# One network, three repeated patterns rewritten: the modulation products, the norm ahead of a product, and the experts' loop

## The reference

```python
# first block, per layer l (x and, in layer 0, also ctx)
sh1, sc1, gt1, sh2, sc2, gt2 = split(silu(c) @ w_ada[l] + b_ada[l], 6)   # w_ada: 1024 x 6144
h = rms_norm(x, g_mix[l]) * (1 + sc1) + sh1
q, k, v, fourier_part, ... = split(h @ w_in[l])
o = concat(global_attention, fourier_mix, window_attention)
x = x + gt1 * (o @ w_out[l])
x = x + gt2 * swiglu(rms_norm(x, g_ffn[l]) * (1 + sc2) + sh2)            # d_ff 2816
...
x = rms_norm(x, g_final)
# second block: an even layer (differential attention, SSM, swiglu) and an odd one
# (two attentions, then a mixture of 8 experts, 2 per token):
for e in range(8):
    out += gates[:, e] * ((silu(t @ w_gate[e]) * (t @ w_up[e])) @ w_down[e])   # t = rms_norm(x, gain)
```

## Time and profile before

| | us |
|---|---|
| median of 3 runs | 3140.36 (3136.24 to 3140.94) |
| the profiled execution, its own time | 3135.54 |
| span in the profile | 3133.8 |
| PE busy | 2664.2 (85%) |
| VectorE busy | 1994.3 (64%) |
| ScalarE busy | 1071.9 (34%) |
| GpSimd busy | 201.4 (6%) |
| weights and other data moved | 543.16 MB, 173 GB/s on average |

### The profile page before, as it was taken

The page is one execution under the profiler, slowest core; times in us unless marked ns, Lnnn a source line. Parts: engine busy times, 40 slices in busy tenths (PEclk is TensorE's granted clock), DMA queues, the critical chain, the costliest instruction groups (busy, mean ns, idle before and its releaser), DMA issues. The chain is left out here.

```text
span 3133.8 us, 50194 instructions
## 1 busy us (share of the span) xinstructions
PE 2664.2 (85%) x18684; PEld 2400.9 (77%) x18684; DVE 1994.3 (64%) x3414; ACT 1071.9 (34%) x1804; POOL 201.4 (6%) x179
## 2 busy tenths in 40 slices
PE   7778898799776889686379966757999999999999
PEld 4667897699565779685379965547988988988988
DVE  6555776577764577755857744654666666666665
ACT  5333444344442444231134421221322322322322
POOL 0050000000004000061000040000000000000000
PEclk9889999899897999896589985577999999999999
DMA  9422352255562134340034440002877877877876
GB/s 354 172 81 82 130 187 106 88 185 190 192 231 76 69 144 184 126 149 14 0 122 181 173 146 1 1 32 91 320 277 274 318 276 277 317 276 277 319 272 224
DMA packets 57195, 543.16 MB, mean 173 GB/s; under 512 B 6584, under 2 KB 6904, under 8 KB 9080
## 3 DMA queue, kind: packets, MB, share of 16 engines
q1 hardware_dynamic: 53840, 529.55, 46.0%
q10 hardware_dynamic: 3248, 12.17, 1.1%
HBM read 540.55 MB, written 1.15 MB: 173 GB/s over the span
## 5 line engine op out<-in xcount | busy, mean ns | idle before, releaser
L2040 PEld LDWEIGHTS bank<-projc,ring 128*128 128x128 f32 x5632 | 654.6, 192 | 17.6 <-issue 4.5
L2040 PE MATMUL bank<-projc,ring 128*128 128x128 f32 x5632 | 655.8, 275 | 1.0 <-DVE projc L2122 1.0
L571 PE MATMUL bank<-src_hi,w_hi 128*128 128x256 f32 x1472 | 420.3, 286 | 29.4 <-DVE w_lo L844 28.2
L791 ACT ACTIVATE w_hi<-ring 128x1024 fp32r<-128x1024 f32 x264 | 278.7, 1059 | 419.8 <-PE bank L573 415.6
L572 PE MATMUL bank<-src_lo,w_hi 128*128 128x256 f32 x1472 | 419.2, 285 | 0.0
L573 PE MATMUL bank<-src_hi,w_lo 128*128 128x256 f32 x1472 | 418.9, 285 | 0.0
L844 DVE TENSOR_TENSOR w_lo<-ring,w_hi 128x1024 fp32r<-128x1024 f32 x264 | 321.7, 1220 | 100.3 <-ACT w_hi L791 99.0
L571 PE MATMUL bank<-w_hi,src_hi 128*128 128x256 f32 x896 | 268.6, 300 | 77.8 <-DVE w_lo L700 69.0
L571 PE MATMUL bank<-w_hi,act_hi 128*128 128x512 f32 x704 | 292.8, 416 | 23.5 <-DVE w_lo L844 12.5
L571 PEld LDWEIGHTS bank<-src_hi,w_hi 128*128 128x128 f32 x1472 | 285.0, 194 | 35.4 <-DVE w_lo L844 30.3
L572 PEld LDWEIGHTS bank<-src_lo,w_hi 128*128 128x128 f32 x1472 | 285.2, 194 | 3.1
(11 more groups left out here) (335 smaller groups left out, 4212.5 us busy)
## 6 DMA issues: line engine op xcount, KB each, us to landing
ring<-in_moe SPq DMA_DIRECT2D x176, 1536.0 KB, 8.4
ring<-in_ffn SPq DMA_DIRECT2D x66, 1536.0 KB, 6.4
ring<-in_w_ada SPq DMA_DIRECT2D x48, 1024.0 KB, 4.9
ring<-in_ffn_ev SPq DMA_DIRECT2D x22, 1536.0 KB, 6.4
ring<-in_w_in SPq DMA_DIRECT2D x18, 1024.0 KB, 4.8
ring<-in_w_out SPq DMA_DIRECT2D x12, 1024.0 KB, 4.8
ring<-in_ev_in SPq DMA_DIRECT2D x12, 1024.0 KB, 4.8
ring<-in_od_in SPq DMA_DIRECT2D x7, 1024.0 KB, 4.7
```

What stands on the lines that cost most here:

```text
L571: pe.matmul(out, ah, bh, start=start and i == 0, stop=False, skip_group_check=True)
L791: act.activation(p.wH[:, kind, :], piece(c, kind), ACT.Copy).then_inc(p.w_hi[kind].sem, 1)
L2040: mm = pe.matmul(p.ps[2 + k % 2][:, u * P:u * P + P], w[:, kt, :], hJ[:, k // FC, kt, :], start=kt == 0, stop=kt == KT - 1)
```

## The change

**Modulation.** The two rows become two of 32 stationary columns (`wide`, the other 30 are zero) and are multiplied with the ring's weights in plain float32, 8 products a chunk and no split. The products for k and k + 4 add into output partitions 32j to 32j + 31 (j = k mod 4). The four partial sums are copied to SBUF, in turn by VectorE and ScalarE, and added by a product with a 0/1 matrix (`sums`) that also turns them into columns. The two gates are formed as rows at the end, 512 columns at a time, and stored to DRAM for the broadcast.

**Norm with product.** `norm_src`, `fourier` and `turn` ahead of a product go into the program of `linear` or `ffn` as its front (`Normed`, `Turned`). The first two weight pieces are split in between; scaling is shared by VectorE and ScalarE; the first chunk's products wait for one slice of the source at a time. The final norm of the first block goes into the next front. GpSimd's work beside a `linear` uses other scratch space and follows the root directly.

**Experts.** Gate and up become split products: tokens stationary, 256 weight columns moving (host layout changed), 24 a chunk. Their result has tokens on partitions, so a transpose (L2223) is added ahead of `down`. The high parts of all three weight pieces are made on ScalarE and the remainders on VectorE; there are two sets of split weights. silu is formed with tanh, two multiplications. `down` lags `up` by two chunks. The output copy, scatter, picks and gather of a job change are spread over the steps of the next (or the same) job. The norm's gain is multiplied into the tokens by GpSimd beside the routing. A chunk comes as two transfers, gate and up (1 MiB) and down (0.5 MiB), each freed by its own remainders. The loop's body is a pair of jobs, 44 chunks written out; the first and the last job stand outside it.

```diff
 def adaln(p, l, loads):
+    wide = p.work[:, 0:KT * 32].rearrange("p (k j) -> p k j", k=KT)
...
-                mm = products(pe, p.ps[c % 2][0:2, 0:PC],
-                              [((scH[:, 4 * h + k, :], scL[:, 4 * h + k, :]), (w[0][:, k, :], w[1][:, k, :]))
-                               for k in range(4)], h == 0, h == 1)
+                for k in range(KT):
+                    j = k % 4
+                    mm = pe.matmul(p.ps[c % 4][32 * j:32 * j + 32, 0:PC], wide[:, k, :], w[:, k, :],
+                                   start=k < 4, stop=k >= 4)
...
+                pe.wait_ge(*ready(c + 1))
+                pe.sem_inc(p.slot_free.sem, 1)
...
+def normed_dve(p, dve, f, split):
...
+    dve.tensor_scalar(p.xn[:, 0, :], f.rows[:, 0, :], st[:, 0:1], None, ALU.mult).then_inc(normed.sem, 1)
+    split(0)
+    for j in (0, 2):
+        dve.wait_ge(*turned(j + 1))
+        for k in (2 * j, 2 * j + 1):
+            dve.tensor_scalar(h[:, k, :], ...).then_inc(kept_v.sem, 1)
+    for k in range(4):
+        low(k)
+    split(1)
+    for k in range(4, KT):
+        low(k)
...
 def linear(...)
+            for i, k in enumerate(front.order):
+                if k // 4 not in [j // 4 for j in front.order[:i]]:
+                    pe.wait_ge(*p.w_lo[k // 4](1))
+                pe.wait_ge(*src_ready(front.ready[i]))
+                for m in range(2):
+                    mm = product(0, k, m, i == 0, i == KT - 1)
...
 def moe(p):
+    sets = ((p.wH, p.wL), (p.wH2, p.wL2))
...
+            def up(i, k):
+                hs = slice((k // FC % 2) * P, (k // FC % 2) * P + P)
+                for half in range(2):
+                    wh, wl = [v[:, half, :].rearrange("p (k n) -> p k n", k=4) for v in sets[k % 2]]
+                    pe.wait_ge(*at(p.w_lo[half], i, k + 1))
+                    mm = products(pe, p.ps[2 + k % 2][:, 0:2 * P],
+                                  [((p.srcH[:, 4 * half + q, hs], p.srcL[:, 4 * half + q, hs]),
+                                    (wh[:, q, :], wl[:, q, :])) for q in range(4)], half == 0, half == 1)
+                    mm.then_inc(p.w_used[half].sem, 1)
...
+            def step(i, b, r, first, last):        # TensorE
+                k = b * FC + r
...
+                    up(i, k)
+                if there(r, 1, first):
+                    turn_act(i, k - 1, first and r == 1)
...
+                if there(r, 2, first):
+                    down(i, k - 2)
+                if r == 1 and not first:
+                    turn_weights(i, b - 1)
+                if 4 <= r < 8 and not first:
+                    scatter(i, b - 1, r - 4)
+                if 10 <= r < 12 and not last:
...
+                    gather(i, b + 1, r - 10)
```

More of the change, by code:

```diff
@@ L467, in rope, with __init__ @@
     chain(dve.tensor_tensor(src, a, b, ALU.add))
[L470 to L476 removed]
+class Normed:
+    def __init__(self, rows, scale, bias=None, banks=(4, 5, 6, 7), final=None):
+        self.rows, self.scale, self.bias, self.banks, self.final = rows, scale, bias, banks, final
+        self.order, self.ready = tuple(range(KT)), tuple(range(1, KT + 1))
+        self.stats = 2 if final is not None else 1
@@ new lines, with __init__, h_tiles @@
+class Turned:
+    def __init__(self, groups, mix=None):
+        self.groups, self.mix = groups, mix
+        ks = [k0 + i for sources, k0 in groups for i in range(len(sources) // NT)]
+        self.order = tuple(ks) + (() if mix is None else (3, 4))
+        counts = [j + 1 for j, (sources, _) in enumerate(groups) for _ in range(len(sources) // NT)]
+        self.ready = tuple(counts) + (() if mix is None else (len(groups) + 1, len(groups) + 2))
+def h_tiles(p):
+    return p.work[:, 0:KT * T].rearrange("p (k t) -> p k t", k=KT)
@@ new lines, in front_begins, with front_passed @@
+def front_begins(p, f):
+    f.root0 = p.rstd.base
+def front_passed(p, f):
+    normed, squared, turned, kept_v, kept_a, hi, lo, final = front_signals(p)
+    if isinstance(f, Normed):
+        normed.passed(NT)
+        squared.passed(f.stats)
+        final.passed(NT if f.final is not None else 0)
+        kept_v.passed(4)
+        kept_a.passed(4)
+        turned.passed(4)
+    else:
+        turned.passed(len(f.groups))
+        if f.mix is not None:
+            for s in mix_signals(p):
+                s.passed(2)
+    hi.passed(f.ready[-1])
+    lo.passed(f.ready[-1])
@@ L616, in side_product, with linear @@
     return mm
-def linear(p, src, n_tok, n_feat=0, out=None, out_feat=None, residual=None, gate=None, side=None,
-           out_at=None, loads=(), beside=None):
+def linear(p, front, n_tok, n_feat=0, out=None, out_feat=None, residual=None, gate=None, side=None,
+           out_at=None, loads=(), front_loads=(), beside=None, split=False):
     nc = p.nc
@@ L646, in _, with high @@
         def _(act):
-            if src is not None:
-                split_src_hi(p, act, src)
-            for q in range(2 * n):
-                if q == 3:
-                    start_loads(p, act, loads)
+            def high(q):
                 g, b = g0 + q // 2, q % 3
@@ L705, in split @@
                     dve.sem_inc(p.slot_free.sem, 1)
[L707 to L708 removed]
+            (normed_dve if is_norm else turned_dve)(p, dve, front, low)
+            for q in range(2, min(4, 2 * n)):
+                low(q)
             for c in range(n):
@@ new lines, in side_piece, with down_piece, walk @@
+    def side_piece(k, half):
+        return p.ring[:, (g0 + k) % RING, half * PIECE:(half + 1) * PIECE]
+    def down_piece(k):
+        return p.ring[:, (g0 + k) % RING, DOWN * PIECE:(DOWN + 1) * PIECE]
+    def walk(eng, between, step):
+        for r in range(FC):
+            step(0, 0, r, True, False)
+        with eng.Fori(0, between) as i:
+            for b in (1, 2):
+                for r in range(FC):
+                    step(i, b, r, False, False)
+        for r in range(FC + 3):
+            step(between, 1, r, False, True)
@@ L1985, in moe, with there @@
+    def there(r, lag, first):
+        return r - lag < FC and not (first and r < lag)
     with nc.Block(no_gpsimd_drain=True) as block:
@@ L2170, in moe @@
+            make_pick(0, 0)
+            for part in range(2):
+                keep_rest(0, 0, part)
+            walk(dve, between, step)
     p.end_stream()
 def odd_layer(p):
-    norm_src(p, p.x, p.col("od_mix"))
     w1 = [v.rearrange("p a d -> p (a d)")[0:HD, :].rearrange("p (i j) -> p i j", i=32) for v in (p.gates[:], p.ctx[:])]
```

947 lines of the change are left out of this document (524 added, 423 removed).

## The result

| | before | after |
|---|---|---|
| median of the runs (lowest to highest) | 3139.45 us (3136.24 to 3140.94) | 2967.95 us (2960.61 to 2969.38) |
| ratio, 95% interval | 1 | 0.945 (0.9433 to 0.9468) |
| span of the profiled execution | 3133.8 us | 2967.6 us |

The account below looks back on a forecast made before the run. PE's own time and the holes in it were taken to bound the kernel. Experts 68, modulation 38 and norms with products 98 sum to 204 us off 3135.5: 2931, said as 2933 us, range 2890 to 3015.

Parts of the forecast that it names:

- Experts: 68 forecast: Experts: 73 us from eight jobs, less 2 for start-up and 3 for jumps back, 68 us faster, between 0 and 75.
- The chunk: Experts: PE takes 4.66 us a chunk against 4.96 before, from split products 2.88, transpose 0.23, down products 1.47, switch 0.08.
- the transpose: Experts: one transpose added per chunk, 0.23 us, taken as 3.67 / 16 from a norm's transposes.
- The change of job: Experts: 7.6 us of PE stays per job and 2.6 us of waits go; VectorE's additions fit in its slack.
- The jump back: Experts' loop of 44 written-out chunks: goes back three times at 1 us each, bounded between nothing and 8.4 us a turn.
- Rival (c): Experts: chunk set by a ScalarE, VectorE and PE ring or VectorE's full durations, 4.9 to 5.1 us; 2975 to 3010; chance 0.16.
- (d): Experts: the halves' transfers end up one at a time; 306 us more, 3239 us, slower; chance 0.04.
- Modulation: 38 forecast: Both modulations: column groups run together without splitting, 14 us won in the first and 24 in the second, together 38.
- (b): Modulation: column groups run one by one, 4.1 us a chunk; 38 becomes -43, 3014 us; chance 0.14.
- the pace of a chunk: Modulation: PE needs 0.85 us a chunk, 1.7 at half clock, so the transfer sets 2.47 us.
- Seams: 98 forecast: Norms or turns into products: ten places 60 us, plus 2, Fourier 18, turns 11, final norm 6, router 1; between 60 and 115.
- a Fourier front: Norm stages with a Fourier part ahead of the product: first chunk ends about 6 us earlier, three places, 18 us.

Follow-up runs that it names:

- adds_later: Against the changed kernel: the four additions of a job's scatter come one step later on VectorE; 2885.99 us.
- no_turn: Against the changed kernel: the experts' loop over pairs of jobs is written out three times, for this input's eight jobs alone; 2947.38 us.
- extra_vector: Against adds_later: VectorE makes two unused 128 x 128 copies more per chunk of the experts; 2889.88 us.
- one_group: Against the changed kernel: all eight products of a modulation chunk go to the first column group, as one sum; 3033.75 us.
- warm: Against the changed kernel: modulation's turning products stand ahead of PE's wait, plus three unused full-array products in chunks 2 to 19; 2960.95 us.
- same_group: Against the changed kernel: a modulation chunk's eight products go to the column groups in the order 0 0 1 1 2 2 3 3; 2965.49 us.

## Why the prediction was right, and where it was off

**Experts: 68 forecast, 29.5 measured.** Three terms were mis-sized, of both signs.

The chunk is 4.33 and not 4.66 us, which is worth 176 x 0.33 = 58 us more. 0.20 of the 0.33 is the transpose: its 0.23 us came from the earlier trace rows, a norm's transposes, where the granted clock is 0.50 (in this kernel too, the row of 90 to 96 us). In the experts it is 1.00 and the transpose adds 0.03. The clock explains some 0.12 of the 0.20, since at 1.00 two transposes in a row start 0.11 us apart (0.38 us for both, 0.27 for one); the rest is that a lone transpose between products costs less than one in a row of transposes. 0.08 was the price of a switch of kind, which doesn't show, and 0.05 the spacing.

The change of job was forecast as 7.6 us of PE with all waits gone, since the additions "come one per step and fit in its 0.6 us of slack". The 7.6 us and the fit are right, once the additions come a step later, as adds_later shows: 102.80 - 22 x 4.33 = 7.5 us. In the changed kernel it is 114.03 - 95.3 = 18.8. The step that failed is this one: it compared sums per chunk, and did not follow what VectorE's addition waits for and what stands behind it in VectorE's order. It cost 11.2 us a job by the marks, and 82 us in all by adds_later (seven jobs have such a scatter).

The jump back was priced at 1 us for each of three, within bounds of 0 and 8.4. Two happen (the third time round the loop ends, and the job that follows takes 114.96), and each costs 10.3 by no_turn and 10.2 by the marks of adds_later, outside the bounds. It isn't one wait but three effects in a row: that of ScalarE, which PE gets to feel, PE's own, and the lower clock that follows. Together 68 + 58 - 82 - 18 = 26, against 29.5.

The Trainium skill, in Runtime: NRT & Kernel Launch (Instruction fetch mechanics), says that a taken branch whose target is no longer held must fetch it before execution goes on, and that most engines hold 512 instructions and PE 2048. The trace agrees: 3.95 us on ScalarE and 5.25 on PE, with nothing to wait for but the crowded instruction packets shown above. It deserved more weight in the forecast than the nearest rows, which were of a loop with a short body.

Rival (c), a chunk set by VectorE at its full durations or by a ring of engines, is refuted for plain chunks: extra_vector shows VectorE's step at 4.00 us, near the forecast's 3 x 1.14 + 3 x 0.21, and PE has no hole in them. A ring did set the pace, but only in the four steps with a scatter (7.50 us). (d) is refuted by the transfers, which carry 355 GB/s in the steady state, where PE never waits.

**Modulation: 38 forecast, 27.3 measured.** The mechanism held: the four column groups run at once, one_group shows it, and (b) falls. The same trial prices (b): 3034 us measured against 3014 forecast. Of the two pages of the Trainium skill that the prediction set against each other, the trace agrees with TensorEngine Tiling (Key Properties), by which different tiles load and multiply in parallel: 1.07 us against 3.64. It does not bear out the sentence of TensorE: Matmul & The Clock Gate (Part 3, The mechanism) that a weight load overlaps running products only when the row group differs: here all groups have the same rows, and the weight load at 801.36 us runs while products that started at 801.15 to 801.17 still do. The term that was off is the pace of a chunk, 2.47 us by the transfer; measured 3.03 by PE in most of the stage. I had reckoned 1.7 us at the half clock for the eight products. The half clock came, and they take 1.93. But I had left out the two turning products behind them (0.92 to the next product's start) and PE's wait for its own end (0.18), though both stand in the code, and though the price of (b) has 0.7 us for them: 1.93 + 0.18 + 0.92 = 3.03.

**Seams: 98 forecast, 109.4 measured.** The forecast steps are seen: the first remainder under the transposes, the first product 4.4 us after the first transpose, the first chunk done after 10.4 us. From one mark to the next (a norm's transposes, the first products of attention or of a Fourier part) the stretches with one norm gain 4.5 to 9.6 us, against 6. The three with a Fourier front gain 9.4, 9.1 and 8.1, together 26.5 where 18 were forecast, which is most of the excess of 11. The final norm and the norm in front of it together gain 14.1. Which step of the Fourier fronts was worth more than its forecast is not taken apart.

**In all:** 166.2 us of span against 204. Of the experts' errors one, +58, covers over half of the other two, -100, and the seams' excess covers the modulation's shortfall. That the time came within 35 us of the forecast owes something to this luck: the experts' waits and jumps were missed by 100 us.

## What to carry to other kernels

When work is spread over the steps of a software pipeline, ask of each piece not only whether the engine has the time, but which other engine's step it waits for: an engine that runs a step ahead loses its lead at every instruction that follows the other too closely, and one step later it is free (82 us here, for two changed numbers). Price the jump back of a long loop body by the engines one after the other; a body of some thousand instructions cost 10 us a turn. Take a duration from rows with the same granted clock and the same neighbours as the place where it is used: a transpose cost 0.23 us in a row of its kind at 0.50, 0.11 at 1.00, and 0.03 alone between other products. And when the pace of a stage is summed up, put in every product that the code issues there.

## What the runs showed of the hardware

Products with 32 stationary columns left PE at the lower of its two clocks: from 778 to 800 us PE was busy 20.08 of 22 us, and the granted clock was 0.50. With three full-width products more per chunk (warm) the same stretch has 1.00. In the first modulation of the changed kernel the same two spacings are seen (1.93 and 1.07 us for sixteen rows). Up to 59.9 us its trace has no record of the clock, so the 1.00 that is printed there says nothing.

Two sets of products to the same column group, one right behind the other, cost nothing as long as the other groups have work too (1.09 us for sixteen rows in same_group, 1.07 in the changed kernel); all in one group they cost 3.4 times as much.
